# The first gather of a mixture-of-experts stage: unscaled rows, clears on another engine, and filler products around the router

## The reference, cut to what matters

```python
def rmsnorm(x, g):
    y = xf * lax.rsqrt(jnp.mean(xf * xf, axis=-1, keepdims=True) + EPS)
    return y * g

def moe(xn, w_router, w_gate, w_up, w_down):
    logits = xn @ w_router
    top_val, top_idx = lax.top_k(logits, TOP_K)          # 2 of 8
    gates = sum(one_hot(top_idx) * softmax(top_val))
    hh = silu(xs @ w_gate[e]) * (xs @ w_up[e]) * gate     # per expert e
    return sum over e of hh @ w_down[e]

    h = h + swa_sink(...)         # second attention, output product and bias
    xn = rmsnorm(h, g_ffn[l])
    h = h + moe(xn, ...)
return rmsnorm(h, g_final)
```

## Time and profile before

| | us |
|---|---|
| median of 3 runs | 1287.51 |
| the runs | 1285.98 to 1290.56 |
| the profiled execution, own time | 1288.11 |
| its span in the profile | 1286.3 |
| mean granted TensorE clock | 0.989 |

### The profile page before, as it was taken

One profiled execution on the slowest core, in us unless ns is written; L12 is line 12 of the kernel. 1 busy time (PEld: TensorE's weight loads), 2 busy tenths in 40 slices (PEclk: granted clock), 3 DMA queues, 4 the chain that ended last, 5 costly groups with the idle time before them and its releaser, 6 DMA issues.

```text
span 1286.3 us, 20295 instructions
## 1 busy us (share of the span) xinstructions
PE 1220.9 (95%) x8367; PEld 621.0 (48%) x8368; DVE 320.9 (25%) x728; ACT 248.7 (19%) x438; POOL 27.9 (2%) x44
## 2 busy tenths in 40 slices
PE   6989999999899999899999998899999999999997
PEld 4755777778665534233433433433343343334333
DVE  2363666667363400100010010010001101000102
ACT  2251434333153111021001111102100210211111
POOL 2100000000110100000000000000000000000000
PEclk9999999999999899999999999999999999999999
DMA  9511645326621699999989999999999999999993
GB/s 339 211 66 67 253 142 192 131 100 236 262 105 68 256 423 423 419 418 411 362 330 426 423 420 422 425 419 419 426 419 409 424 423 418 422 423 382 392 427 130
DMA packets 73169, 413.71 MB, mean 322 GB/s; under 512 B 6607, under 2 KB 11853, under 8 KB 64637
## 3 DMA queue, kind: packets, MB, share of 16 engines
q1 hardware_dynamic: 71708, 409.59, 79.0%
q0 software_dynamic: 1088, 1.81, 0.4%
q10 hardware_dynamic: 288, 1.05, 0.2%
HBM read 411.38 MB, written 1.05 MB: 321 GB/s over the span
## 4 chain that ended last, share of the span: by engine, by line
PE 82%; DMA 5%; DVE 4%; SPq 3%; issue 3%; ACT 2%; POOL 0%; DVEq 0%; ACTq 0%; POOLq 0%
PE ps L1427 14%; PE ps L1407 11%; PE ps L1494 8%; PE ps L1402 6%; PE ps L1385 6%; PE ps L1107 4%; PE ps L1111 4%; PE ps L1108 4%; SPq L647 3%; PE ps L1389 3%; PE ps L1478 3%; PE ps L1376 3%; PE ps L1458 2%; DMA ring<-in_moe_w_up 2%; PE ps L1280 2%
## 5 line engine op out<-in xcount | busy, mean ns | idle before, releaser
L1427 PE MATMUL ps<-ring,arena 128*64 128x448 f32 x640 | 252.2, 545 | 9.5 <-DMA ring<-in_moe_w_up 5.7
L1428 PE MATMUL ps<-ring,arena 128*64 128x448 f32 x640 | 253.6, 548 | 7.3 <-issue 7.3
L1407 PE MATMUL ps<-ring,arena 128*32 128x448 f32 x1152 | 162.7, 543 | 0.0
L1408 PE MATMUL ps<-ring,arena 128*32 128x448 f32 x384 | 161.3, 543 | 0.0
L1427 PEld LDWEIGHTS ps<-ring,arena 128*64 128x64 f32 x640 | 83.9, 137 | 152.4 <-issue 139.7
L1976 DVE TENSOR_TENSOR arena<-arena,ps 64x448 f32<-64x448 f32 (+1 forms) x64 | 38.5, 613 | 377.2 <-ACT arena L892 198.4
L1494 PE MATMUL ps<-ring,arena 128*64 128x512 f32 x280 | 124.7, 595 | 3.3 <-DMA ring<-in_moe_w_down 3.3
L1495 PE MATMUL ps<-ring,arena 128*64 128x512 f32 x280 | 124.7, 595 | 0.0
L1402 PE MATMUL ps<-ring,arena 128*32 128x448 f32 x768 | 90.8, 544 | 8.6 <-DVE arena L1976 4.0
L1407 PEld LDWEIGHTS ps<-ring,arena 128*32 128x32 f32 x1152 | 48.1, 111 | 94.8 <-issue 94.8
L1710 DVE TENSOR_TENSOR w_lo<-ring,w_hi 128x2048 fp32r<-128x2048 f32 x33 | 75.6, 2292 | 62.1 <-ACT w_hi L784 60.6
(11 more groups left out here) (297 smaller groups left out, 1433.1 us busy)
## 6 DMA issues: line engine op xcount, KB each, us to landing
ring<-in_moe_w_down SPq DMA_DIRECT2D x64, 1792.0 KB, 17.7
ring<-in_moe_w_gate SPq DMA_DIRECT2D x127, 896.0 KB, 15.0
ring<-in_moe_w_up SPq DMA_DIRECT2D x127, 896.0 KB, 16.1
ring<-in_ffn_w_gate SPq DMA_DIRECT2D x5, 2048.0 KB, 7.7
ring<-in_ffn_w_up SPq DMA_DIRECT2D x5, 2048.0 KB, 7.8
ring<-in_ffn_w_down SPq DMA_DIRECT2D x5, 2048.0 KB, 8.1
ring<-in_mla_w_o SPq DMA_DIRECT2D x2, 2048.0 KB, 24.2
ring<-in_swa_w_q SPq DMA_DIRECT2D x2, 2048.0 KB, 8.3
```

The costliest lines, as they stand in the source:

```text
L1407: pe.matmul(ps[32 * j:32 * j + 32, c, 0:CH], thirds[j], wu[:, c * CH:(c + 1) * CH], start=first, stop=last)
L1408: mm = pe.matmul(ps[SLOTS:P, c, 0:CH], thirds[2], wg[:, c * CH:(c + 1) * CH], start=first, stop=last)
L1427: pe.matmul(ps[0:NARROW, c, 0:CH], lhs, wu[:, cols], start=(k == 0), stop=(k == KD - 1))
L1428: mm = pe.matmul(ps[64:64 + NARROW, c, 0:CH], lhs, wg[:, cols], start=(k == 0), stop=(k == KD - 1))
```

## The change

Six things, all around the routing:

1. The gather reads unscaled rows. ScalarE copies `h` to `xn` behind its squares, and the norm's factor per token (`stat[:, 4 + t]`) is multiplied into `sel` (in the first gather and in each item's). The gain goes into the copies out of PSUM, as a factor per partition: four ScalarE operations of 128x96 in place of one copy of 128x384, and a `tensor_tensor` in place of a copy on VectorE. `grow` and its load are gone, and so are the two operations that made the normed rows.
2. The five memsets move from VectorE to GpSimd (`cleared`).
3. The router's products have 64 columns: `wr` gets seven more columns of experts' blocks, which are zero, and each product takes eight blocks of it. Only the first eight columns of a result are used.
4. A filler product of 256 columns (the identity by constants, `keep_busy`) stands ahead of the last `h_to_T`.
5. Fillers of 512 and 384 columns stand behind the last router product, ahead of the wait for the mask.
6. The constants get 96 more columns (`C_NEXT`, 1 to 96), so that `sel` needs no addition of 1.

```diff
             pool.wait_ge(s.sv_mm, 2)
             pool.dma_start(bo_row, swa_b_o[0:1, :].to_broadcast([P, D])).then_inc(s.rel_loaded, 16)
-            pool.dma_start(grow, g_ffn[1:2, :].to_broadcast([P, D])).then_inc(s.rel_loaded, 16)
-            pool.wait_ge(s.rel_loaded, 16 * 10)
+            pool.wait_ge(s.rel_loaded, 16 * 9)
...
+            pool.wait_ge(s.swo_mm, 2)
+            for v in (slots[:, :, ITEMS_MAX:ITEMS_MAX + 1], ):
+                nc.gpsimd.memset(v, -1.0).then_inc(s.cleared, 1)
+            for v in (gates[:, :, ITEMS_MAX:ITEMS_MAX + 1], ysb[:], sgt[:], hh[:]):
+                nc.gpsimd.memset(v, 0.0).then_inc(s.cleared, 1)
             rstd_rows()
...
                 act.wait_ge(s.h_attn1, 2 * t + 2)
-                squares(t)
+                act.activation(hhT[:].rearrange("p a j n -> p (a j n)")[:, 0:D], h[:, t, :], ACT.Square,
+                               accum_out=stat[:, t:t + 1]).then_inc(s.ssq_ready, 1)
+                act.copy(xn[:, t, :], h[:, t, :]).then_inc(s.xn_ready, 1)
...
             act.wait_ge(s.gath_first, 2)
-            act.copy(xgT[:, 0:4, :].rearrange("p k n -> p (k n)"), ps[:, GATHER_BANK, 0:4 * SLOTS]).then_inc(s.xgT_ready_v, 1)
+            for j in range(4):
+                ins = act.activation(xgT[:, j, :], ps[:, GATHER_BANK, j * SLOTS:(j + 1) * SLOTS], ACT.Copy, scale=gcol(V_GF1, j))
+            ins.then_inc(s.xgT_ready_v, 1)
...
+            def keep_busy(bank, n):
+
+                pe.matmul(ps[:, bank, 0:n], ident, cst[:, 0:n], start=True, stop=True)
+
...
-                    mm = pe.matmul(ps[:, 2, t * NE:(t + 1) * NE], xT[:, k, t * P:(t + 1) * P], wr[:, k, :], start=(k == 0), stop=(k == KD - 1))
+                    mm = pe.matmul(ps[:, 2, t * KD * NE:(t + 1) * KD * NE], xT[:, k, t * P:(t + 1) * P],
+                                   wr[:, k:k + KD, :].rearrange("p k n -> p (k n)"), start=(k == 0), stop=(k == KD - 1))
...
             router(1, 0)
+            keep_busy(5, 256)
             h_to_T(1, 1)
             router(1, 1)
+            keep_busy(7, 512)
+            keep_busy(7, 384)
...
             pe.wait_ge(s.sel_ready, 3)
+            pe.wait_ge(s.xn_ready, 8)
             gather()
...
             add_out(1, s.swo_mm, s.h_attn1, SWO_BANK)
-            norm_rows(0, grow)
             add_out(2, s.swo_mm, s.h_attn1, SWO_BANK)
             evac_hT(0, 0)
             evac_hT(0, 1)
+            mean_squares(2, 0, D)
             evac_hT(1, 0)
-            dve.memset(ysb[:], 0.0).then_inc(s.y_last, 1)
-            dve.memset(sgt[:], 0.0).then_inc(s.y_last, 1)
-            dve.memset(hh[:], 0.0).then_inc(s.y_last, 1)
...
             add_out(3, s.swo_mm, s.h_attn1, SWO_BANK)
             evac_hT(1, 1)
             mean_squares(3, 1, D)
+            dve.wait_ge(s.cleared, 5)
...
             dve.wait_ge(s.rstd_ready, norms[0])
-            dve.scalar_tensor_tensor(out=xn[:, 1, :], in0=h[:, 1, :], scalar=stat[:, 5:6], in1=grow,
-                                     op0=ALU.mult, op1=ALU.mult).then_inc(s.xn_ready, 1)
...
-                dve.tensor_scalar(sel[:, t, :], cst[:, C_IOTA:C_IOTA + SLOTS], 1.0, cum[:, t, 0:1], ALU.add, ALU.is_equal).then_inc(s.sel_ready, 1)
+                dve.tensor_scalar(sel[:, t, :], cst[:, C_NEXT:C_NEXT + SLOTS], cum[:, t, 0:1], stat[:, 4 + t:5 + t], ALU.is_equal, ALU.mult).then_inc(s.sel_ready, 1)
...
-                dve.tensor_copy(xgT[:, 0:4, :].rearrange("p k n -> p (k n)"), ps[:, GATHER_BANK, 0:4 * SLOTS]).then_inc(s.xgT_ready_v, 1)
+                dve.tensor_tensor(xgT[:, 0:4, :], ps[:, GATHER_BANK, 0:4 * SLOTS].rearrange("p (k n) -> p k n", k=4),
+                                  vecT[:, V_GF1:V_GF1 + 4].unsqueeze(2).to_broadcast([P, 4, SLOTS]), ALU.mult).then_inc(s.xgT_ready_v, 1)
```

More of the change, by code:

```diff
@@ L84 @@
 C_MH = C_INV + HALF
-C_N = C_MH + TT
+C_NEXT = C_MH + TT
+C_N = C_NEXT + SLOTS
 V_GA0, V_GF0, V_GA1, V_KVG, V_GQ, V_GKV, V_KVB, V_BQ = 0, 8, 16, 24, 32, 35, 37, 38
@@ L119, in constants @@
     c[:, C_MH:C_MH + TT] = -0.5
+    c[:, C_NEXT:C_NEXT + SLOTS] = np.arange(SLOTS) + 1
     return c
@@ L245, in __init__ @@
         self.y_last = sem("y_last")
+        self.cleared = sem("cleared")
         self.sel_ready = sem("sel_ready")
@@ L289, in build @@
         stat = sb("stat", [P, 16])
-        wr = sb("wr", [P, KD, NE])
+        wr = sb("wr", [P, 2 * KD - 1, NE])
         kvb_row = sb("kvb_row", [1, P])
@@ L381, in build @@
         spT = carve(4 * 3 * P, "p (k n) -> p k n", k=4)
-        grow = carve(D)
         assert used[0] <= BIAS0
@@ L672, in _ @@
                 (kvb_row[:], kv_b[P:2 * P].rearrange("(a n) -> a n", a=1)),
-                (wr[:], w_router[0].rearrange("(k p) e -> p k e", p=P)),
+                (wr[:, 0:KD, :], w_router[0].rearrange("(k p) e -> p k e", p=P)),
                 (sinks_h[:], swa_sinks[0:1, :].to_broadcast([P, AH])),
@@ L908, in _, with upper_xgT @@
             act.sem_inc(s.sgt_ready, 1)
+            def upper_xgT(n):
+                for j in range(4):
+                    ins = act.activation(xgT[:, 4 + j, :], ps[:, GATHER_BANK + 1, j * SLOTS:(j + 1) * SLOTS], ACT.Copy, scale=gcol(V_GF1, 4 + j))
+                ins.then_inc(s.xgT_ready_a, n)
             act.wait_ge(s.gath_first, 2)
-            act.copy(xgT[:, 0:4, :].rearrange("p k n -> p (k n)"), ps[:, GATHER_BANK, 0:4 * SLOTS]).then_inc(s.xgT_ready_v, 1)
+            for j in range(4):
+                ins = act.activation(xgT[:, j, :], ps[:, GATHER_BANK, j * SLOTS:(j + 1) * SLOTS], ACT.Copy, scale=gcol(V_GF1, j))
+            ins.then_inc(s.xgT_ready_v, 1)
             act.wait_ge(s.gath_mm, 2)
-            act.copy(xgT[:, 4:8, :].rearrange("p k n -> p (k n)"), ps[:, GATHER_BANK + 1, 0:4 * SLOTS]).then_inc(s.xgT_ready_a, 2)
+            upper_xgT(2)
             act.wait_ge(s.counts_ready, 1)
@@ L924, in act_item @@
                 act.wait_ge(s.gath_mm, i + 3)
-                act.copy(xgT[:, 4:8, :].rearrange("p k n -> p (k n)"), ps[:, GATHER_BANK + 1, 0:4 * SLOTS]).then_inc(s.xgT_ready_a, 1)
+                upper_xgT(1)
                 act.wait_ge(s.down_mm, i * (2 * TILES) + (2 * TILES + 1))
@@ L1682, in _ @@
             dve.wait_ge(s.biasrows_loaded, 16 * 12)
-            link(dve.tensor_tensor(wr[:], wr[:], vecT[:, V_GF1:V_GF1 + KD].unsqueeze(2).to_broadcast([P, KD, NE]), ALU.mult))
+            dve.memset(wr[:, KD:2 * KD - 1, :], 0.0).then_inc(s.y_last, 1)
+            link(dve.tensor_tensor(wr[:, 0:KD, :], wr[:, 0:KD, :], vecT[:, V_GF1:V_GF1 + KD].unsqueeze(2).to_broadcast([P, KD, NE]), ALU.mult))
             link(dve.tensor_copy(posq[:], posq_i[:]))
@@ L1847, in _ @@
             dve.wait_ge(s.bo_added, 2)
-            dve.wait_ge(s.rel_loaded, 16 * 10)
             def evac_hT(t, half):
@@ L1871, in _ @@
             mean_squares(3, 1, D)
+            dve.wait_ge(s.cleared, 5)
+            for q in (s.sel_ready, s.selg_ready, s.hh_ready, s.y_ready_v, s.xgT_ready_v, s.h_added):
+                dve.sem_inc(q, 1)
             lg, mask, top, idx = (rt[:, :, 8 * n:8 * n + 8] for n in range(4))
@@ L1876, in _ @@
             dve.wait_ge(s.router_mm, 2)
-            link(dve.tensor_copy(lg, ps[:, 2, 0:TT * NE].rearrange("p (t n) -> p t n", t=TT)))
+            link(dve.tensor_copy(lg, ps[:, 2, 0:TT * KD * NE].rearrange("p (t k n) -> p t k n", t=TT, k=KD)[:, :, 0, :]))
             dve.max(top[:, 0, :], lg[:, 0, :])
@@ L1969, in dve_item @@
                 for t in range(TT):
-                    dve.tensor_scalar(sel[:, t, :], iota, slots[:, t, bass.ds(i + 1, 1)], None, ALU.is_equal).then_inc(s.sel_ready, 1)
+                    dve.tensor_scalar(sel[:, t, :], iota, slots[:, t, bass.ds(i + 1, 1)], stat[:, 4 + t:5 + t], ALU.is_equal, ALU.mult).then_inc(s.sel_ready, 1)
                 for n in range(8):
@@ L1993, in _ @@
                 add_rows(items, j)
-            dve.wait_ge(s.rel_loaded, 16 * 11)
+            dve.wait_ge(s.rel_loaded, 16 * 10)
             for t in range(TT):
```

## The result

The changed kernel takes **1277.66 us** (median of 6 runs, 1276.40 to 1279.46) against 1286.74 for the kernel before beside it (6 runs, 1283.45 to 1290.56): ratio 0.9937, 95% interval 0.9919 to 0.9955. It is 9 us faster, 0.6%. The forecast was 1289.0 with a range down to 1286.0, and it gave this side 4 chances in 100. It was wrong.

A forecast was written before the change was run, and what follows sets the result against it. It took TensorE to bound the kernel, the first item waiting for the counts; -0.05 us for its start and +1.5 for the clock gave +1.45, 1289.0 us on the median, no measurable change; range 1286.0 to 1291.5.

The forecast's parts named there:

- Fourth, that wait: TensorE's wait of 3.6 us between the faster first gather and the first item, charged +1.5 us for a fallen clock.
- The sum: All terms together: -0.05 us for the first product's start plus 1.5 for the clock, +1.45 us.
- Right: Signs at the first item: gather 3.7 us at clock 1.00, pause 3 to 4, product 2.4 behind counts, low stretch 3.4.
- The gather does decide: Rival: the first item starts 0.37 us behind its gather, at 431.6; -3.2 us with constants, 1284.3 us; chance 0.08.
- One microsecond at the first item is one of the kernel: A shift at the first item's start is carried in full to the kernel's end.
- The mask comes 0.48 us later: Ahead of the first gather: +0.43 us for the 256-column filler, +0.05 for router products of 64 columns.
- From the mask to line 1902: From TensorE's mask start to line 1902: 2.34 us becomes 1.59 at the upper clock (-0.75), plus 0.12 for `sel`'s second factor.
- The path over the counts decides: The first item waits for the counts: 4.94 us of unchanged work from line 1902, then 2.41 us to the first product.
- The constants: At the kernel's start: 8% more columns on a 6.3 us transfer delay TensorE's start by +0.1 us.
- The clock behind the pause: After the first item's wait, 3.4 us of its dense products run at the lower clock: +1.5 us, between 0 and 1.7.
- The bound 1.7: Upper limit in us of the clock's cost at the first item: half of a 3.4 us low stretch.
- the rival of a long stretch: Rival: 9.5 us of the first item's products run at half rate, +4.7 us, 1292.2 us; chance 0.08.

The follow-up runs named there:

- The hold: The changed kernel with four more dummies of 512 columns between the first gather and the wait for the counts: 1273.26 us, ratio 0.9895.
- experiments 2 and 3: 2: changed kernel plus 243 unused semaphore increments, 1314.51 us (1286.6 less 27.9 us of later start); 3: changed kernel without its three fillers, 1286.58 us.
- with 80: The kernel before with 80 increments of an unused semaphore at the head of TensorE's program: 1297.57 us, ratio 1.0098.

## Why the prediction was wrong

**The step that failed** is the list of terms itself. "Fourth, that wait" closes it, and "The sum" has no term for where TensorE's code lies after 13 more instructions. That term was -13.6 us in the profiles, four times all others. The prediction had the trace of it in hand: it quotes the pause of 2.47 us at 968.41, but only as a witness on the clock. It never asked what TensorE waited for there, though nothing in the profile did release it, though the like of it stood three times in one place, and though the change touches what instructions lie ahead of it. All signs that it named as "Right" stand at the first item, so they could come true beside a wrong time. None of its rivals had the term either: the one that lay nearest in time, "The gather does decide" (1284.3), is not what happened, since the item started 4.2 us behind the gather.

**One microsecond at the first item is one of the kernel**: borne out by the medians. The hold's 3.6 us between the first two gathers stand beside 4.4 us in the medians, and 5.4 us by the ratios to the kernel before (0.9895 against 0.9937). In the two profiled executions only 1.9 us of them are left from the first gather to the end (838.9 against 840.8); another 1.6 went in item 3.

**The mask comes 0.48 us later**: 7.09 against 6.56 us from the router's first product, +0.53. Right.

**From the mask to line 1902**: forecast 1.59 + 0.12 = 1.71, measured 425.66 - 424.09 = 1.57. Right; the fillers held the clock at 1.00 there.

**The path over the counts decides**: right. From line 1921 to the end of 1953 it took 4.93 us, as the 4.94 before. Behind the counts the first product came after 3.17 us instead of 2.41. The sequencer's rows show where most of the 0.76 lie:

```profile
L1554 PEldq MOVE  x1: 29/29/29, 431.5 to 431.5; - x1
L1554 PEldq BRANCH_PREFETCH_HINT  x1: 55/55/55, 432.2 to 432.2; - x1
```

Between two neighbours at the loop's head 0.67 us pass, where they stood 0.1 apart before. It goes with the edge's place: in the kernel before with the head 17, 14 and 9 in front of it this gap is 1.26, 1.05 and 0.70 us, and it is 0.1 in every run with a head 21 or more away. No packet of the instruction queue lies in it, so what is waited for there is not shown. So the first product shifts by +0.51 and not by -0.05; without the 0.76 it would be -0.25.

**The constants**, +0.1: not to be told. TensorE's first product came at 10.3 us against 9.5, but at 8.8, 8.9 and 9.9 in three other runs with the same constants.

**The clock behind the pause**, +1.5 between 0 and 1.7: right in kind, too small. The low stretch lasted from 432.8 to 439.6, twice the 3.4 us of the one at 526. Of it 5.8 us lay in the item's products, from 433.76, and it cost half of that, 2.9 us (74.5 - 71.6). The bound 1.7 was no bound; the rival of a long stretch, 9.5 us and +4.7, was too long. The Trainium skill ("TensorE: Matmul & The Clock Gate", section on HAM oscillation), cited in the prediction for a clock that falls in such a wait, agrees with this run.

So the sum of +1.45 was +3.4 in the profiled executions (0.5 for the start, 2.9 for the clock). With the layout left as it was the change gains nothing: nearest to it are the runs of experiments 2 and 3 (1286.6 both, against 1285.6).

## What to carry to other kernels

Where a long loop body with branches runs on an engine, any edit that changes the number of instructions ahead of it can be worth up to about 1%, of either sign: the ratios here run from 0.9937 to 1.0098 by empty instructions alone (3.6 us of the latter are overrun at the start). Measure an edit against the kernel before at equal layout (pad both with empty instructions), or its effect is not known: this change looked like a gain of 9 us and, against the kernel before with 13 increments, is none. Both have the ratio 0.9937, and from the first gather to the end the changed kernel took 840.8 us, where the kernel before took 837.7, 840.2 and 840.4 with 13, 8 and 5. A pause that the profile puts down to "issue", in one place and behind a far jump, is the sign, and a packet of the instruction queue that ends shortly before the engine goes on speaks for it; a few empty instructions in an idle stretch are the cure, if the head, the last branch and the exit of the loop are looked at. And a gather made faster in front of a fixed wait wants dummies behind it, not only ahead of it.

## What the runs showed of the hardware

- A pause of 1.4 to 2.9 us (nine of them, in three runs) where a block's edge lies 21 or 22 instructions behind the target of a far jump back; 2.1 to 2.7 at the jump if the branch stands 54 behind an edge, 4.4 to 5.4 if it stands 6 behind. With the low clock behind it, an item loses up to 7.8 us (101.3 against 93.5).
- In 18 such pauses TensorE goes on 1.3 to 1.6 us behind the end of a 16 KB packet of the instruction queue.
- A loop body of some 914 instructions is run again without any such packet (none begins between 731.47 and 851.23 us of the kernel before).
- The exit of the loop can stop as well: 4.18 us, and 6.0 us (26.1 against 20.1) from the last gather to the end.
- 243 semaphore increments in a row take 38.2 us from the span's start, so at most 157 ns each.
- The length of a pause does not tell that of the low stretch behind it. Low stretches of 6.8 us stand behind pauses of 4.16 (changed kernel), 3.63 (kernel before with 5) and 4.46 and 5.35 us (with 80), ones of 3.4 us behind 2.31, 3.7 and 4.39 us, and behind the 2.47 us at 968.41 there is none.
